# Two norms with three begun tiles and seven weight buffers, and sigmoids set apart from logarithms, in a transformer kernel

## The reference, cut to what matters

```python
def rms_norm(x, g):
    y = x * lax.rsqrt(jnp.mean(x * x, axis=-1, keepdims=True) + 1e-5)
    return y * g

def first_block(x, ...):
    xn = rms_norm(x, mix_norm)                       # norm 0
    proj = xn @ w_in + b_in                          # q, k, v, conv and gate columns
    ...                                              # attention, convolution, gates -> merged
    h = x + merged @ w_out
    hn = rms_norm(h, ffn_norm)                       # norm 1
    up = causal_depthwise_conv(hn @ w_up, ffn_conv_w)  # 44 tiles of 128 features
    gate, val = split(up)
    h = h + (silu(gate) * val) @ w_down
    return rms_norm(h, final_norm)                   # norm 2

def second_block(x, ...):
    h = x @ w_in_2                                   # 33 slots of weights
    ...
    # hgrn2: q, f, i of six heads of 64
    log_f = logaddexp(log(max(lb, 1e-30)), log1p(-lb) + log_sigmoid(f))
    key = (1 - lb) * sigmoid(-f)                     # cumulative sums of log_f, exp of differences
    o_hg = o_hg * rsqrt(mean(o_hg ** 2) + 1e-6)
    # stick breaking, four heads: log_sigmoid of the scores, reversed sums, exp
    log_rest = where(mask, log_sigmoid(-z), 0)
    a = exp(log_sigmoid(z) + sums of log_rest)
    # nsa: gates = sigmoid(h[gate columns]), three softmax branches
    ...                                              # output projection, layer norm
```

## Time and profile before

| | |
|---|---|
| Median of 3 runs (lowest, highest) | 1154.02 us (1150.44, 1156.69) |
| Profiled execution, own time | 1157.58 us |
| its span | 1155.3 us |
| Busy: PE, PEld, DVE, ACT, POOL | 1089.7, 864.1, 588.9, 470.0, 39.9 us |
| Share of the chain that ended last: PE, issue, DVE, ACT | 79%, 7%, 7%, 4% |
| Traffic | 105.49 MB, mean 91 GB/s |

### The profile page before, as it was taken

How to read it: one execution, slowest core, us unless ns; L and a number is a source line. 1 busy time by engine, 2 the same in 40 slices (tenths; PEclk the granted TensorE clock), 3 DMA queues, 4 the chain that set the end, 5 groups by cost and what they waited for, 6 DMA issues and landing times.

```text
span 1155.3 us, 13978 instructions
## 1 busy us (share of the span) xinstructions
PE 1089.7 (94%) x5476; PEld 864.1 (75%) x5476; DVE 588.9 (51%) x1130; ACT 470.0 (41%) x843; POOL 39.9 (3%) x49
## 2 busy tenths in 40 slices
PE   4999999999989999999999998899999889999894
PEld 4887788888877888888888877797776656666583
DVE  4346644333355666434666534426685643566744
ACT  4334432223344444213344323625336336555622
POOL 0000000000010000000000002000000001000004
PEclk9999999999999999999999998899999889999997
DMA  6312222232324633332232322432121123311011
GB/s 233 105 61 61 68 73 91 91 110 91 112 75 159 233 102 95 100 100 91 91 99 102 99 84 74 158 104 87 40 64 37 37 64 104 134 56 37 19 37 73
DMA packets 28624, 105.49 MB, mean 91 GB/s; under 512 B 3226, under 2 KB 3386, under 8 KB 27920
## 3 DMA queue, kind: packets, MB, share of 16 engines
q1 hardware_dynamic: 24576, 85.15, 22.4%
q0 software_dynamic: 3696, 18.42, 4.6%
q10 hardware_dynamic: 288, 1.05, 0.2%
HBM read 99.86 MB, written 7.36 MB: 93 GB/s over the span
## 4 chain that ended last, share of the span: by engine, by line
PE 79%; issue 7%; DVE 7%; ACT 4%; DMA 1%; POOL 0%; POOLq 0%; ACTq 0%; DVEq 0%
PE ps L629 24%; PE ps L631 22%; PE ps L630 22%; PE ps L976 1%; ACT whi L1038 1%; PE ps L993 1%; DVE wlo L1379 1%; PE ps L1010 1%; PE ps L739 1%; ACT A L1305 1%; PE ps L713 1%; DMA GR<-brow 1%; PE ps L724 1%; PE ps L873 1%; PE ps L958 1%
## 5 line engine op out<-in xcount | busy, mean ns | idle before, releaser
L629 PE MATMUL ps<-XH,whi 128*128 128x512 f32 (+1 forms) x864 | 341.7, 396 | 15.4 <-DVE XL L1414 7.7
L1379 DVE TENSOR_TENSOR wlo<-raw,whi 128x1024 fp32r<-128x1024 f32 (+2 forms) x159 | 191.2, 1205 | 289.5 <-ACT whi L1038 289.2
L631 PE MATMUL ps<-XH,wlo 128*128 128x512 f32 (+1 forms) x864 | 330.9, 383 | 0.0
L630 PE MATMUL ps<-XL,whi 128*128 128x512 f32 (+1 forms) x864 | 330.6, 383 | 0.0
L1038 ACT CAST whi<-raw 128x1024 fp32r<-128x1024 f32 (+2 forms) x159 | 162.8, 1026 | 132.6 <-PE ps L631 130.0
L629 PEld LDWEIGHTS ps<-XH,whi 128*128 128x128 f32 x864 | 166.2, 192 | 55.5 <-issue 18.2
L631 PEld LDWEIGHTS ps<-XH,wlo 128*128 128x128 f32 x864 | 166.2, 192 | 31.5
L630 PEld LDWEIGHTS ps<-XL,whi 128*128 128x128 f32 x864 | 166.4, 193 | 27.7 <-issue 0.2
L629 PE MATMUL ps<-whi,GH 128*128 128x512 f32 x176 | 69.1, 393 | 1.4 <-ACT ps L1050 1.1
L630 PE MATMUL ps<-wlo,GH 128*128 128x512 f32 x176 | 68.5, 389 | 0.0
L631 PE MATMUL ps<-whi,GL 128*128 128x512 f32 x176 | 68.5, 389 | 0.0
(11 more groups left out here) (251 smaller groups left out, 1366.8 us busy)
## 6 DMA issues: line engine op xcount, KB each, us to landing
raw<-wp SPq DMA_DIRECT2D x151, 512.0 KB, 3.4
vec_dram<-row_dram POOLq DMA_DIRECT2D x1, 3072.0 KB, 12.4
x_dram<-H POOLq DMA_DIRECT2D x1, 2048.0 KB, 8.7
A<-w1c POOLq DMA_DIRECT2D x2, 1024.0 KB, 8.3
A<-x_dram POOLq DMA_DIRECT2D x1, 2048.0 KB, 12.3
y<-A SPq DMA_DIRECT2D x8, 256.0 KB, 2.0
raw<-wp SPq DMA_DIRECT2D x4, 402.0 KB, 3.1
A<-vec_dram POOLq DMA_DIRECT2D x1, 1536.0 KB, 9.2
```

The costliest lines, as they stand in the source:

```text
L629: self.e.matmul(o, ah, bh, start=start, stop=False)
L630: self.e.matmul(o, ah, bl, start=False, stop=False)
L631: return self.e.matmul(o, al, bh, start=False, stop=stop)
L1379: self.e.tensor_tensor(wlo[i % NR][:, 0:w], raw[i % NR][:, 0:w], whi[i % NR][:, 0:w].bitcast(F), ALU.subtract).then_inc(sems["lo"], 1)
```

## The change

1. Seven buffers of split weights in place of three. They are used six in a ring from slot 50 to 116, the seventh for slot 117, then 3, 4, 5 for slots 118 to 120, and three in a ring after that (`BUF`, `PREV`). The raw buffers stay three.
2. At norms 1 and 2 the splits of the next slots stand ahead of the rows (`split_all` before `rows_normed`), the rows of norm 2 join three slots in place of two, and turns take banks (4, 5) and (3, 6) in turn, so that a turn waits for the XL of two turns earlier, and for the squares in the bank that it takes over. The order is rows 0, 1, 2, turn 0, turn 1, rows 3, turn 2.
3. `first_three` begins three tiles in place of two.
4. The lower bound's small exp goes ahead of the gates of block one (`lower`).
5. `hf` takes all sigmoids, `hl` afterwards the three logarithms. The gates' sigmoid becomes an exp, with an addition and a reciprocal on DVE, and the explicit load of the set with exp and ln at that place (L1218) is gone.
6. Regions in SBUF are moved to make room; two memsets and three loads on POOL wait for other events.

The diff, cut to its core:

```diff
+NORM_BANKS = [(4, 5), (3, 6), (4, 5), (3, 6)]
+LAST_DOWN = SLOT_B2 - 1
+BUF = [i % NR for i in range(SLOT_FFN)]
+BUF += [(2 + n) % 6 for n in range(LAST_DOWN - SLOT_FFN)] + [6] + [3, 4, 5]
+BUF += [i % NR for i in range(N_SLOTS - len(BUF))]
+PREV = [max([j for j in range(i) if BUF[j] == BUF[i]], default=-1) for i in range(N_SLOTS)]
...
+    def rows_normed(m, rows):
+        for t in range(3):
+            rows(t)
+            if t == 2:
+                en.turn(m, 0)
+            en.norm_rest(m, t)
+        en.turn(m, 1)
+        rows(3)
+        en.norm_rest(m, 3)
+        en.turn(m, 2)
+
+    def first_three(m, i, tile, tiles):
+        en.part(i, 0, 0)
+        en.turn(m, 3)
+        en.part(i, 1, 0)
+        en.part(i, 2, 0)
+        en.split_all(i + 4)
+        for n in range(3):
+            en.part(i, n, 1)
+            tile(*tiles[n])
+            if n == 1:
+                en.split_all(i + 5)
...
+    en.split_all(SLOT_FFN + 4)
+    rows_normed(1, lambda t: en.wout(1, 3, t))
...
+                if half == 1 and c == 1:
+                    en.split_all(i + 4 + g)
...
+    rows_normed(2, lambda t: en.down(1, 1, 5, t))
     en.block2()
-    first_two(2, B2_HGF, en.hf, [(0, 4), (1, 4)])
+    first_three(2, B2_HGF, en.hf, [(0, 4), (1, 4), (2, 4)])
     en.block2_after()
-    slot(B2_HGF + 2)
-    for part in range(4):
-        en.hf(2, part)
+    for i in range(3):
+        en.hl(i)
...
-                    self.wait_ge("xl", 8 * m + 2 * (t - 1) + c + 1)
+                    if t > 1:
+                        self.wait_ge("xl", 8 * m + 2 * (t - 2) + c + 1)
+                    elif m:
+                        self.wait_ge("sq", sums_at(m, t + 1, 1))
...
             def split(self, i):
                 self.wait_ge(f"w{i % NR}", 16 * (i // NR + 1))
-                self.wait_ge("used", i - NR + 1)
+                self.wait_ge("used", PREV[i] + 1)
...
             def hf(self, i, part):
-                self.wait_ge("sc", 4 * (i - 2) + 4)
-                self.e.activation(T1[:, u, :], p[:, :], ACT.Sigmoid).then_inc(sems["fa"], 1)
+                self.e.activation(HG[:, i, 2, :], p[:, :], ACT.Sigmoid).then_inc(sems["fa"], 1)
                 self.e.activation(HG[:, i, 1, :], p[:, :], ACT.Sigmoid, scale=-1.0).then_inc(sems["fb"], 1)
+
+            def hl(self, i):
+                self.wait_ge("sc", 4 * (i - 2) + 4)
...
-                        self.e.activation(gates, gates, ACT.Sigmoid).then_inc(sems["hgt"], 1)
-                        self.e.preload_act_table_set(LNEXP)
+                        self.e.activation(gates, gates, ACT.Exp, scale=-1.0).then_inc(sems["hgt"], 1)
...
+                self.e.tensor_scalar(gates, gates, 1.0, None, ALU.add).then_inc(sems["n_cf"], 1)
+                self.wait_ge("n_cf", 1)
+                self.e.reciprocal(gates, gates).then_inc(sems["n_cf"], 1)
```

More of the change, by code:

```diff
@@ L96, with ring @@
 TILES = {}
-def ring(banks, tiles):
-    busy = {}
+def ring(banks, tiles, busy=None):
+    busy = {} if busy is None else busy
     for n, (i, j, name, value) in enumerate(tiles):
@@ L156 @@
     q = k = v = qk = soft = tr = cp = pv = fin = ft = cc = cx = cb = gate = branch = merge = wout = idle
[L157 to L158 removed]
+    distances = biases = ffn = lower = up = glu = down = block2 = idle
+    hf = hl = hq = hi = av = src = nk = nq = sq = sk = z = idle
     h_start = h_diag = h_q1 = h_prep = h_mult = h_off = h_prod = h_pick = h_pv = h_norm = idle
@@ L264, in stages @@
     weave(conv(), (attention(), 0, 19 / 24))
+    en.lower()
     for n in range(8):
@@ L275, in stages @@
     for c in range(2):
[L276 to L280, removed]
+        for g in range(4 if c == 0 else 2):
+            slot(SLOT_WOUT + 4 * c + g)
             for t in range(4):
                 en.wout(c, g, t)
[L283 to L286, removed]
+    en.split_all(SLOT_FFN + 4)
+    rows_normed(1, lambda t: en.wout(1, 3, t))
     en.ffn()
@@ L291, in stages @@
             if half == 0 and j == 0:
-                first_two(1, SLOT_FFN, en.up, [(0, 0, 0, 2), (0, 0, 1, 2)])
+                first_three(1, SLOT_FFN, en.up, [(0, 0, 0, 2), (0, 0, 1, 2), (0, 1, 0, 2)])
                 en.distances()
             else:
-                for g in range(2):
+                for g in range(1 if half == 0 and j == 1 else 0, 2):
                     slot(SLOT_FFN + half * N_HALF + 2 * j + g)
@@ L304, in stages @@
         for c in range(2):
[L305 to L309, removed]
+            for g in range(6 if half == 0 or c == 0 else 3):
+                i = SLOT_FFN + half * N_HALF + 22 + 6 * c + g
+                slot(i)
+                if half == 1 and c == 1:
+                    en.split_all(i + 4 + g)
                 for t in range(4):
                     en.down(half, c, g, t)
[L312 to L315, removed]
+    rows_normed(2, lambda t: en.down(1, 1, 5, t))
     en.block2()
-    first_two(2, B2_HGF, en.hf, [(0, 4), (1, 4)])
+    first_three(2, B2_HGF, en.hf, [(0, 4), (1, 4), (2, 4)])
     en.block2_after()
-    slot(B2_HGF + 2)
-    for part in range(4):
-        en.hf(2, part)
+    for i in range(3):
+        en.hl(i)
     for i in range(3):
@@ L529, in program @@
         FN = sb("FN", [P, D], F, p2)
-        VE = sb("VE", [6, 1024], F, p2)
+        pv = ExitStack()
+        VE = sb("VE", [6, 1024], F, pv)
+        pv.close()
+        hi6 = sb("whi6", [P, S], FR, p2)
+        lo6 = sb("wlo6", [P, S], FR, p2)
+        for i in range(3, 6):
+            whi.append(sb(f"whi{i}", [P, 1024], FR, p2))
+            wlo.append(sb(f"wlo{i}", [P, 1024], FR, p2))
+        whi.append(hi6)
+        wlo.append(lo6)
         LM, EX, LB, OML, LBF = (st[:, 32 + 3 * i:35 + 3 * i] for i in range(5))
@@ L799, in down @@
                     self.wait_ge("sq", sums_at(2, t, 0))
-                for gg in ((4, 5) if half == 1 and c == 1 and g == 5 else (g,)):
+                for gg in ((3, 4, 5) if half == 1 and c == 1 and g == 5 else (g,)):
                     self.rows(SLOT_FFN + half * N_HALF + 22 + 6 * c + gg, t, GH, GL, 512, 2 * gg,
```

92 lines of the change are left out of this document (56 added, 36 removed).

## The result

The changed kernel takes 1163.11 us, median of 9 runs, against 1153.62 us of the kernel before (9 runs): ratio 1.0069, interval 1.0044 to 1.0094, 0.7% slower. The forecast was 1163.

A forecast was written before the change was run, and what follows sets the result against it. PE's queue was taken as the bound, busy 1089.7 of 1155.3 us. Terms -14.0, +2.0, -0.5, +21.6 and +0.2 gave +9.3 on a median of 1154.0: 1163 us; 8-in-10 range 1149 to 1175, likeliest case 1158 to 1168.

The forecast's parts named there:

- Norm 2 stretch: From three w_down slots' rows through four turns and three tiles: 36.0 us in place of 50.0, -14.0.
- Norm 1: Four splits ahead of the first addition delay it behind a DMA; PE idles before two turns: +2.0, 0 to +4.5.
- Start: At norm 0, turn 1 no longer waits for the XL of turn 0: -0.5 us, 0 to -1.1.
- Gates and all behind head 3: Two more small DVE instructions in front of the first nsa tile: +0.2 us, 0 to +0.5.
- All but the loads: Everything in the forecast except the function-set loads and their clock cost: -12.3 us.
- Loads, waits: Stick breaking, heads 0 to 2: 24 function-set loads count except for ACT's idle time, +19.6 us (12 to 33.3).
- Loads, clock: After PE's new idle pieces in heads 0 to 2, part of what follows runs at the lower clock: +2.0 us.
- Loads together: Waits for function-set loads in heads 0 to 2 plus the lower clock after them: +21.6 us.
- A: Rival, chance 0.12: the loads hide in ACT's idle time, only about 5 us counts; 1147 us, faster.
- C: Rival, chance 0.07: norm 2's gain mostly fails, raw buffers still three and splits waiting on a landing; -5, 1172 us.
- D: Rival (0.18): norm 2 -15, loads 14, about 1155 us; last section: distance from norm 1's turn 0 into head 0.
- B: Rival, chance 0.13: all loads exposed, PE at 1.2 GHz in more gaps; 33 + 4, 1169 to 1170, up to 1175.

The follow-up runs named there:

- second execution: The changed kernel once more, unedited, profiled again: 1162.70 us, the median of its runs being 1162.66; the first profiled execution took 1157.94.
- one-line version: The changed kernel with the explicit load of the exp and ln set put back behind the gates' Exp, 25 loads fewer: 1136.17 us, ratio 0.9844.

## Why the prediction was right, point by point

| Term | Predicted | Measured |
|---|---|---|
| Norm 2 stretch | -14.0 | 49.95 to 36.06: -13.9 |
| Feed-forward part ahead of it | 0 | -2.1 |
| Norm 1 | +2.0 | +1.6 and +1.1 (first, second execution) |
| Start | -0.5 | -0.9 and -1.75 |
| Gates and all behind head 3 | +0.2 | +0.4 |
| All but the loads, by the one-line version | -12.3 | 1136.17 - 1152.47 = -16.3 |
| Loads, waits | +19.6 | +14.8 |
| Loads, clock | +2.0 | +12.4 |
| Loads together | +21.6 | +27.1 in the trace, 27 and 26 in the runs |
| Sum | +9.3 | +9.5 |

The rows of the loads set the second execution against the one-line version.

- **Norm 2: right, with its mechanism.** Stretch, clock and the pieces under 1 us came as written. The runs say what in it counts, which the prediction left open: early splits 5.8 us by the medians and 7.5 in the trace, second pair of banks 2.7, third begun tile nothing, grouped sigmoids nothing. The rest of the 14, joined rows and the order, wasn't taken apart.
- **The step that I left out** is what the seven buffers do ahead of norm 2. Two short waits of PE stood in the trace of before and are gone:

```profile
498.39 0.50 PE L629 MATMUL ps<-whi,GH 128*128 128x512 f32 x1 [0.33 <-DVE H L1511]
...
679.29 0.50 PE L629 MATMUL ps<-whi,GH 128*128 128x512 f32 x1 [1.09 <-ACT ps L1050]
```

  An addition stood there behind a split that waited for PE to release a buffer: the cast of before runs at 675.58 after 4.39 us for PE, the first square only at 678.52; now the first square is at 677.06 with no cast ahead. 1.4 of the 2.1 us are these two; 0.7 I can't assign.
- **Norm 1: right.** 8.0 us to the first addition, waits of 4.72 and 1.92 where I had 4.7 and 2.5, then slow matmuls. One split fewer takes 3.4 us away, which makes the stretch better than before.
- **Start: mis-sized,** -0.5 for up to -1.75. Turn 1's wait of 0.85 us for XL is gone; how much of the rest is the clock, which differs between the two executions, isn't settled.
- **Loads: the mechanism right, both sizes wrong.** The waits were where I put them (the second Exp, DVE behind the Ln) and the heads longer by 10.1, 8.3 and 8.7 us than in the one-line version, where I had 8, 7 and 5. The step that failed is "part of what follows runs at the lower clock: 2.0". It was 12.4. The 2.0 was not worked out from any row; in fact the mean granted clock is 0.90, 0.91 and 0.82 over all three heads. The waits came out smaller than mine, 14.8 for 19.6. Slow matmuls may have filled part of them, but that isn't shown: of the two executions of the changed kernel the one with less busy time in the heads has less idle time as well, 20.5 against 22.8.
- **The trace that I worked from had slow heads itself.** In the profiled execution of before heads 1 and 2 stand at a clock of 0.90, with 5.3 us more busy time in the three heads than in the one-line version (81.91 for 76.57) and the same idle time (8.1 and 8.0). Against that trace the loads cost 111.73 - 89.97 = 21.8 us, 14.7 of waits and 7.0 of clock, beside my 21.6. I took its execution's 3.56 us above the median off the time and not off the heads. No profile of an execution of before near the median exists, so that these 3.56 us lie in the heads is an inference: with heads as in the one-line version it would take an estimated 1157.58 - 5.4 = 1152.2 us, and the medians are 1152.4 to 1153.6.
- At the lower level the clock is half, so a mean of 0.90 says a fifth of the time. By the clocks of the second execution PE stands at the lower level for 2 x 0.10 x 33.80 + 2 x 0.09 x 39.44 + 2 x 0.18 x 38.49 = 27.7 us. The Trainium skill ("TensorE: Matmul & The Clock Gate", section "Terms") takes the loss as that time by one minus the ratio, here half, an estimated 13.9 us. The trace has 12.4 us more busy time; the rule agrees, as an upper figure.
- Loads take 1.28 us each and the next activation begins 0.02 us later, in the heads as in `hf`. The drain that the Trainium skill states ("ScalarE: Activation LUTs", section "What ACT_TABLE_LOAD costs") isn't in this trace.

```profile
845.44 1.28 ACT L1379 ACT_TABLE_LOAD   x1
846.74 0.31 ACT L1379 ACTIVATE H<-H 128x128 f32<-128x128 f32 x1
```

- **Rivals.** A (loads hide) fell, and so did C (norm 2 fails) and D. B had the loads and the clock at 37, too much, but its clock, 4, was nearer than my forecast's, and PE at 1.2 GHz in more of the gaps is what happened. B's time doesn't come out of its terms: 37 in place of 21.6 is 15.4 more than the forecast, 1178 to 1179 us, not 1169 to 1170.
- **Sign of the loads on ACT.** 20 more loads and 24.6 us more busy time came as written (20, 25); the instruction count rose by 20, not 18.

So the whole came out at +9.5 by luck: -4.0 on the side of the norms met +5.5 on that of the loads. The two would make +10.8; the rest is the median of before, which is 1153.62 us in one series and 1152.47 in the next.

## What to carry to other kernels

An edit that removes an explicit load of a function set looks like one instruction saved; read ACT's order behind it as far as the next explicit load, because every change between Ln and Exp then gets a load of its own (here 25 loads and 27 us, which one line gives back). When you cost a stretch of many short waits on the busiest engine, cost the clock too: here it was 8.6 of 21.0 us in one execution and 12.4 of 27.1 in another. Ask of the trace that you work from whether it is a typical execution, and where it is slow. And splitting early pays only up to the raw buffers in hand: three splits ahead of norm 1 did no harm, the fourth put a DMA landing in front of the whole norm.

## What the runs showed of the hardware that I had not expected

The length of the wait just ahead doesn't tell the clock. The same eight matmuls took 2.37 us behind waits of 2.84 and 3.00 us and 4.06 behind 2.83. The clock within the heads changes from one execution of the same program to the next, and with it the time: of nine runs of the changed kernel in the second series two took 1157.6 and 1157.8 us and seven 1161.8 to 1163.6. It isn't only the loads: of the seven profiled kernels with the set loaded by name and seven buffers, two ran all three heads at 1.00 (84.6 us), and five had one or two heads at 0.90 or 0.95 (86.1 to 87.9 us). So differences of 1 to 3 us between single traces' totals can come from the heads, which is why D is given beside the medians. What makes one execution fall to the lower level and the other not stays open.
